# Who makes the low parts of w_out's first three slabs: from VectorE to GpSimd, behind its queries of batches 5 to 7

## The chip, the cores and the metric

One core of a Trainium2 chip runs the whole kernel in one launch. The metric is the device time of that core in microseconds (us), the median of several executions. The engines are TensorE (PE, with its weight loads as PEld), VectorE (DVE), ScalarE (ACT), GpSimd (POOL) and SyncE (SP), which issues the loads from device memory.

## What is computed

A trunk of two layers over 512 prompt tokens and 8 groups of 16 sample tokens (640 rows of 1024). Each layer, cut to what matters here:

```python
h = rms_norm(x, norm_mix); proj = h @ w_in
# o_ret: retention, o_fox: forgetting attention, o_conv: gated short convolution
x = x + concat([o_ret, o_fox, o_conv], -1) @ w_out
x = x + (silu(dwconv3(h2 @ w_gate)) * (h2 @ w_up)) @ w_down      # h2 = rms_norm(x, norm_ffn)

# attention of the sample tokens, for each of 8 batches: 512 cached keys and 16 new ones
sc = einsum('bqhd,bkhd->bhqk', q, k_all) * scale + cq[..., None] - c_t[:, :, None, :]
p = softmax(where(mask, sc, -inf)); o = einsum('bhqk,bkhd->bqhd', p, v_all)
```

## The kernel before, in words

All large products are made of three matmuls (`mm3`): each operand is split into a high part, rounded to fp32r, and a low part, the remainder. Weights arrive in slabs of 128x1024 f32 in three buffers `raw` (slab n in slot n % 3). ACT rounds a slab into `whi` (`split` of ACT, line 1156, semaphore `hi_split`), DVE subtracts that from `raw` into `wlo` (`split` of DVE, line 1538, semaphore `lo_split`), and PE multiplies. Both have `upto(n)`, which makes all slabs up to n that are still missing. SP loads the next slab of a slot when `lo_split` says that the low part of the one before is done. `WO` = 28 is the first of eight slabs of w_out, and `SLOTS` = 3.

The change lies in the sample steps, between the prompt's attention and w_out. For batch n the work goes round the engines:

- POOL, `queries(b, u)`: puts the 16 queries of batch b in block form into `qbd` (two buffers). It waits until the scores of batch b - 2 are complete (`("ss", b - 2)` full).
- PE, `turned(n)`: turns the cached keys of batch n by transposes in four groups of four (`keys_turned`, through three PSUM banks, so the fourth group needs the bank of the first), then the exponentials of batch n - 1 (`ps`), then the remaining part with the output `ob` of batch n - 2. `scores(n)` is the product of `qbd` with the 16 new keys `fkT` and with the 512 turned keys `kT`; `values(n)` is the product of the probabilities of batch n - 1 with the cached values.
- DVE, `step(n)`: two key copies (`key_copy`, L1936) that free PSUM banks; copies out of the bank `po` (L1977, L1981); the masked scores with their running extreme for the old and the new keys (L1997); the smaller of the two extremes (L2001, both operands columns of `small` in SBUF), which releases ACT through `smax`; for the batch before, the sum of the exponentials (L2005), its reciprocal (L2007) and the scaled output `ob` (L2011). In steps 5, 6 and 7 the low part of one slab of w_out follows (lines 2013 to 2015).
- ACT, `step(n)`: two other key copies and the turned probabilities `pTs` (L1252), then the exponentials (L1385). In steps 4, 5 and 6 the high part of one slab of w_out follows.
- SP: cached keys and values of the next batches (1 MB each, lines 757 and 761) as buffers come free, then the slabs of w_out from the fourth on.

`whi` and `wlo` share memory with the cached keys and values of batches 2 and 3 (`kx`, `vx`, `ky`); the wait for `("so", 2)`, the complete output of batch 2, protects that. On PE, `out_slab(0)` follows the steps directly, with the last two `turned` and `values` between the first slabs. The order on each engine is written out by hand and the engines are tied by semaphores. The DVE and ACT lines in question:

```python
if n in (5, 6, 7):                 # DVE, end of step(n)
    B.wait_full(dve, ("so", 2), l)
    upto(WO + n - 5, l)
if n in (4, 5, 6):                 # ACT, end of step(n), behind the exponentials
    B.wait_full(act, ("so", 2), l)
    upto(WO + n - 4, l)
```

Of the kernel before, what the change touches and what calls it, by code (L numbers as in the profile page):

```python
# [30 lines left out]
F32 = mybir.dt.float32  # L31
# [3 lines left out]
ALU = mybir.AluOpType  # L35
# [5 lines left out]
SEQ, NB, NS, PAST = 512, 8, 16, 512  # L41
# [21 lines left out]
SLOTS = 3  # L63


FL, CC, CH, CB, WO, G0 = 4, 22, 24, 26, 28, 36
# [304 lines left out]
def build(nc, a):  # L371
    with ExitStack() as ctx:
        sems = {}

        def sem(name):
            sems[name] = ctx.enter_context(nc.semaphore(name))
            return sems[name]

        bank = [ctx.enter_context(nc.psum_tensor(f"bank{i}", [P, 512], F32)) for i in range(8)]
        B = Banks([sem(f"full{i}") for i in range(8)], [sem(f"free{i}") for i in range(8)])  # L380
# [13 lines left out]
        def own(name, shape, dt=F32):  # L394
            t, top[0] = at(name, shape, dt, top[0])
            return t
# [21 lines left out]
        raw = own("raw", [P, SLOTS, 1024])  # L418
# [70 lines left out]
        def key_home(n, p_):  # L489
            return kT[:, p_, :] if n > 0 else k0[:, p_, :] if p_ < 2 else kT[:, p_ - 2, :]  # L490
# [48 lines left out]
        hi_split = sem("hi_split")  # L539
        lo_split = sem("lo_split")  # L540
# [111 lines left out]
        def slot(n):  # L652
            return n % SLOTS
# [17 lines left out]
        def nth(n, l, more=1):  # L671
            return l * EVENTS + (n if n < DLAST else EV_LAST + n - DLAST) + more
# [26 lines left out]
        def apart(eng):  # L699

            eng.sem_inc(parted, 1)
# [285 lines left out]
        def _(pool):  # L987
# [15 lines left out]
            def norm(which, l):  # L1003
                for t in range(TT):
                    pool.wait_ge(sumsq, l * (2 * TT) + which * TT + t + 1)
                    apart(pool)
                    rsqrt(SS + t, VAR + t, RS + t, 1, 1.0 / D, rstd)

            for l in range(DEPTH):
# [53 lines left out]
                def queries(b, u):  # L1063
                    for par in range(2):
                        dst = qbd[64 * par:64 * par + 64, u, :].rearrange("p (c s) -> p c s", c=4)[:, :, 16 * par:16 * par + 16]
                        src = fqT[64 * par:64 * par + 64, :, SEQ + NS * b:SEQ + NS * b + NS]
                        pool.tensor_copy(dst, src)
                    pool.drain().then_inc(q_ready, 1)
# [12 lines left out]
                for b in range(NB):  # L1081
                    if b >= 2:
                        B.wait_full(pool, ("ss", b - 2), l)
                        apart(pool)
                    queries(b, b % 2)

                norm(1, l)
                pool.wait_ge(cat_lo, l * CATS + CATS)
# [59 lines left out]
        def _(act):  # L1148
            split_to = [0]
# [8 lines left out]
            def upto(n, l):  # L1158

                while split_to[0] <= n:  # L1160
                    if split_to[0] >= SLOTS or l == 0:
                        wait_used(act, split_to[0] - SLOTS, l)
                    elif split_to[0] == 0:
                        B.wait_full(act, ("u", "loop", "a4"), l - 1, PAIRS - 2)
                    else:
                        B.wait_full(act, ("d", "end", split_to[0] - 1, TT - 1), l - 1)
                    split(split_to[0], l)
                    split_to[0] += 1
# [76 lines left out]
            for l in range(DEPTH):  # L1245
                split_to[0] = 0

                def evac(key, out, l, it=None, view=None):

                    B.wait_full(act, key, l, it)  # L1250
                    src = bank[B.bank(key)][:, :] if view is None else view(bank[B.bank(key)])
                    act.activation(out, src, ACT.Copy).then_inc(B.free[B.bank(key)], 1)  # L1252
# [121 lines left out]
                def step(n):  # L1374

                    if n < NB:
                        for p_ in (1, 3) if n > 1 else (2, 3) if n == 1 else ():
                            evac(("kt", n, p_), key_home(n, p_), l)
                    if 1 <= n <= NB:
                        evac(("pt", n - 1), pTs[:, (n - 1) % 2, 0:512], l)  # L1380
                    if n < NB:
                        act.wait_ge(smax, l * NB + n + 1)
                        o = SB + 8 * (n % 2)
                        for c0, n_, acc in ((0, PAST, 3), (PAST + NS * n, NS, 4)):
                            act.activation(ps[:, n % 2, c0:c0 + n_], ps[:, n % 2, c0:c0 + n_], ACT.Exp, scale=-1.0,  # L1385
                                           bias=col(o + 2), accum_out=col(o + acc)).then_inc(sexp, 1)
                    if n in (4, 5, 6):
                        B.wait_full(act, ("so", 2), l)
                        upto(WO + n - 4, l)

                for n in range(STEPS):
                    step(n)
# [135 lines left out]
        def _(dve):  # L1528
            split_to = [0]
# [11 lines left out]
            def upto(n, l):  # L1541
                while split_to[0] <= n:
                    split(split_to[0], l)
                    split_to[0] += 1
# [71 lines left out]
            for l in range(DEPTH):  # L1616
# [348 lines left out]
                def step(n):  # L1965
                    if n < NB:
                        for p_ in (0, 2) if n > 1 else (0, 1) if n == 1 else ():
                            key_copy(n, p_)
                    if n == 1:
                        heads_lo(3)  # L1970
                    if n >= 1:
                        key = ("po", n)
                        bk = bank[B.bank(key)]
                        B.wait_full(dve, key, l)
                        if n <= NB:
                            dve.memset(ps[:, (n - 1) % 2, PAST + NS * (n - 1):PAST + NS * n], 0.0)
                            ins = dve.tensor_copy(pTs[:, (n - 1) % 2, 512:640], bk[:, 0:P])  # L1977
                        if n >= 2:
                            for par in range(2):
                                src = bk[64 * par:64 * par + 64, P:2 * P].rearrange("p (c s) -> p c s", c=4)  # L1980
                                ins = dve.tensor_copy(os_[64 * par:64 * par + 64, :, NS * (n - 2):NS * (n - 1)],  # L1981
                                                      src[:, :, 16 * par:16 * par + 16])
                        ins.then_inc(B.free[B.bank(key)], 1)
                    if n < NB:
                        o = SB + 8 * (n % 2)
                        if n == 0:
                            dve.wait_ge(bnew_ready, l + 1)
                            B.wait_full(dve, ("ss", 0), l)
                            for u in range(2):
                                dve.memset(ps[:, u, PAST:], 0.0)  # L1990
                            dve.drain()
                        for key, c0, n_, c_, bias in ((("ss", n), 0, PAST, 0, pbias[n % 4][:, :]),
                                                      (("sn", n), PAST + NS * n, NS, 1, bnew[:, n, :])):
                            if c_ == 0:
                                dve.wait_ge(pb_in[n % 4], l * 32 + 16 * (n // 4 + 1))
                            B.wait_full(dve, key, l)
                            dve.tensor_tensor_reduce(out=ps[:, n % 2, c0:c0 + n_], in0=bank[B.bank(key)][:, 0:n_], in1=bias,  # L1997
                                                     scale=-1.0, scalar=HUGE, op0=ALU.add, op1=ALU.min,
                                                     accum_out=col(o + c_)).then_inc(B.free[B.bank(key)], 1)
                        dve.drain()  # L2000
                        dve.tensor_tensor(col(o + 2), col(o), col(o + 1), ALU.min).then_inc(smax, 1)  # L2001
                    if 1 <= n <= NB:
                        o = SB + 8 * ((n - 1) % 2)
                        dve.wait_ge(sexp, l * 2 * NB + 2 * n)
                        dve.tensor_tensor(col(o + 5), col(o + 3), col(o + 4), ALU.add)  # L2005
                        dve.drain()
                        dve.reciprocal(col(o + 6), col(o + 5))  # L2007
                        dve.drain()
                        key = ("so", n - 1)
                        B.wait_full(dve, key, l)  # L2010
                        dve.tensor_scalar(ob[:, (n - 1) % 2, :], bank[B.bank(key)][:, 0:P], col(o + 6), None,  # L2011
                                          ALU.mult).then_inc(B.free[B.bank(key)], 1)
                    if n in (5, 6, 7):
                        B.wait_full(dve, ("so", 2), l)
                        upto(WO + n - 5, l)

                for n in range(STEPS):
                    step(n)
# [4 lines left out]
                def add(key, c, t, it=None):  # L2023
# [2 lines left out]
                    dve.tensor_tensor(x[:, t, 512 * c:512 * c + 512], x[:, t, 512 * c:512 * c + 512],  # L2026
                                      bank[B.bank(key)][:, :], ALU.add).then_inc(B.free[B.bank(key)], 1)

                upto(WO + 5, l)
                for t in range(TT):  # L2030
                    add(("wo", 0, t), 0, t)
# [768 lines left out]
```

## Time and profile before

| what | value |
|---|---|
| median of 3 runs | 1594.05 us (1593.94 to 1594.11) |
| profiled execution, its own time | 1593.2 us |
| span of its instructions | 1591.4 us |
| granted TensorE clock | 1.00 |
| PE / PEld busy | 1568.2 us (99%) / 1375.8 us (86%) |
| DVE / ACT / POOL busy | 1073.9 us (67%) / 683.6 us (43%) / 397.8 us (25%) |
| DMA | 168.06 MB, 106 GB/s over the span |

All rows are of one profiled execution; times in them count from the start of its span. The sample steps of layer 1 lie between 266 and 307 us, those of layer 2 between 1054 and 1096 us. Matmuls are pipelined and their ends are modelled, so PE's short waits are read from start times and from the idle time in brackets, not from its busy share. A line number is that of the kernel's code; `split`, `evac` and `mm` are helpers, so their lines serve many places and the names of the tiles tell them apart.

### The profile page before, as it was taken

The numbers are of one execution on the slowest core, as the hardware profiler recorded it, in microseconds if no ns is written. First come the engines' busy times: TensorE is split into PE (matmuls) and PEld (weight loads), VectorE is DVE, ScalarE is ACT, GpSimd is POOL, SyncE is SP. The second block draws the span as 40 slices with busy tenths as digits, with TensorE's granted clock in tenths as the row PEclk, the third lists the DMA queues.
The fourth block names the chain that finished last, engine by engine and source line by source line (L and its number), as shares of the span: only waits on it lengthen the run. The fifth ranks groups of instructions, "written<-read, shape, count | busy, mean of one in ns | idle before, by whom it ended". The sixth has DMA issues, their size and how long they took to land.

```text
span 1591.4 us, 29061 instructions
## 1 busy us (share of the span) xinstructions
PE 1568.2 (99%) x10196; PEld 1375.8 (86%) x10196; DVE 1073.9 (67%) x1847; ACT 683.6 (43%) x1280; POOL 397.8 (25%) x505
## 2 busy tenths in 40 slices
PE   8999999999999999999999999999999999999998
PEld 6878896689999999999888789877899999999997
DVE  4445357539988888888644552674499888878885
ACT  4323337426444444444433233463365444444442
POOL 1113100003433333333112140000043333333330
PEclk9999999999999999999999999999999999999999
DMA  7213455622232222222232225555213222222222
GB/s 233 77 55 84 154 161 193 242 80 67 80 90 82 80 91 88 85 89 67 79 106 67 71 81 183 168 202 198 80 54 118 83 90 80 79 79 79 80 78 72
DMA packets 118872, 168.06 MB, mean 106 GB/s; under 512 B 28261, under 2 KB 80175, under 8 KB 114624
## 3 DMA queue, kind: packets, MB, share of 16 engines
q1 hardware_dynamic: 118648, 166.95, 33.8%
q8 instruction: 49, 0.80, 0.2%
q14 instruction: 29, 0.24, 0.0%
q10 hardware_dynamic: 146, 0.07, 0.0%
HBM read 157.11 MB, written 9.89 MB: 105 GB/s over the span
## 4 chain that ended last, share of the span: by engine, by line
PE 89%; DVE 6%; issue 2%; ACT 1%; DVEq 1%; DMA 0%; POOL 0%; POOLq 0%; SPq 0%; ACTq 0%
PE bank L2239 84%; PE bank L2301 5%; DVE wlo L1552 1%; DVE wlo L1538 1%; DVE x L2026 0%; DVE pf L1898 0%; DVE pf L1911 0%; DVE gact L2056 0%; DVE ps L1997 0%; DVE xn L1590 0%; DVE gulo L1562 0%; DVE xlo L1552 0%; DVE kT L1936 0%; DMA raw<-in_w_up 0%; DMA raw<-in_w_gate 0%
## 5 line engine op out<-in xcount | busy, mean ns | idle before, releaser
L2239 PE MATMUL bank<-whi,hhi 128*128 128x512 f32 x560 | 225.1, 402 | 1.1 <-DVE hlo L1562 0.6
L2239 PE MATMUL bank<-whi,hlo 128*128 128x512 f32 x560 | 219.2, 391 | 0.0
L2239 PE MATMUL bank<-wlo,hhi 128*128 128x512 f32 x560 | 218.7, 390 | 0.0
L2239 PE MATMUL bank<-hhi,whi 128*128 128x320 f32 x640 | 198.7, 310 | 0.8 <-DVE hlo L1562 0.8
L2239 PE MATMUL bank<-hhi,wlo 128*128 128x320 f32 x640 | 197.8, 309 | 0.0
L2239 PE MATMUL bank<-hlo,whi 128*128 128x320 f32 x640 | 197.6, 309 | 0.0
L1538 DVE TENSOR_TENSOR wlo<-raw,whi 128x1024 fp32r<-128x1024 f32 x80 | 100.1, 1251 | 109.6 <-ACT whi L1156 108.2
L2239 PE MATMUL bank<-whi,guhi 128*128 128x512 f32 x440 | 171.7, 390 | 0.4 <-DVE gulo L1562 0.4
L2239 PE MATMUL bank<-wlo,guhi 128*128 128x512 f32 x440 | 171.3, 389 | 0.0
L2239 PE MATMUL bank<-whi,gulo 128*128 128x512 f32 x440 | 171.3, 389 | 0.0
L2026 DVE TENSOR_TENSOR x<-x,bank 128x512 f32<-128x512 f32 x220 | 142.8, 681 | 28.9 <-PE bank L2239 27.0
L2239 PEld LDWEIGHTS bank<-whi,hhi 128*128 128x128 f32 x560 | 105.5, 188 | 25.7 <-issue 3.3
L1156 ACT ACTIVATE whi<-raw 128x1024 fp32r<-128x1024 f32 x80 | 84.4, 1057 | 95.9 <-PE bank L2239 87.3
L2239 PEld LDWEIGHTS bank<-whi,hlo 128*128 128x128 f32 x560 | 105.4, 188 | 22.9
L2239 PEld LDWEIGHTS bank<-wlo,hhi 128*128 128x128 f32 x560 | 105.8, 189 | 20.0
L2239 PEld LDWEIGHTS bank<-hhi,whi 128*128 128x128 f32 x640 | 120.2, 188 | 2.7 <-issue 1.9
L2239 PEld LDWEIGHTS bank<-hlo,whi 128*128 128x128 f32 x640 | 120.2, 188 | 0.8
L2239 PEld LDWEIGHTS bank<-hhi,wlo 128*128 128x128 f32 x640 | 120.1, 188 | 0.0
L1121 POOL TENSOR_TENSOR s<-raw 128x512 f32<-128x512 f32 x60 | 89.8, 1497 | 84.3 <-DMA raw<-in_w_gate 84.3
L1121 POOL TENSOR_TENSOR s<-raw,gains 128x512 f32<-128x512 f32 x20 | 26.9, 1347 | 311.8 <-DMA raw<-in_w_up 301.8
L2239 PEld LDWEIGHTS bank<-whi,gulo 128*128 128x128 f32 x440 | 82.6, 188 | 17.3
L2239 PEld LDWEIGHTS bank<-whi,guhi 128*128 128x128 f32 x440 | 82.6, 188 | 17.3 <-DVE gulo L1562 0.9
(310 smaller groups left out, 3606.4 us busy)
## 6 DMA issues: line engine op xcount, KB each, us to landing
raw<-in_w_in SPq DMA_DIRECT2D x52, 512.0 KB, 3.9
raw<-in_w_gate SPq DMA_DIRECT2D x44, 512.0 KB, 3.8
raw<-in_w_down SPq DMA_DIRECT2D x44, 512.0 KB, 3.5
vb<-in_cache_fox_v SPq DMA_DIRECT2D x14, 1024.0 KB, 6.8
raw<-in_w_up SPq DMA_DIRECT2D x24, 512.0 KB, 3.8
gains<-in_w_up SPq DMA_DIRECT2D x20, 512.0 KB, 3.8
raw<-in_w_out SPq DMA_DIRECT2D x16, 512.0 KB, 4.5
kb<-in_cache_fox_k SPq DMA_DIRECT2D x6, 1024.0 KB, 4.9
```

Of the source, the lines that this page charges most:

```text
L1121: pool.tensor_tensor(by_k(out[:, :]), x_, y_, op).then_inc(s_sum, 1)
L1156: act.activation(whi[:, slot(n), 0:width(n)], raw[:, slot(n), 0:width(n)], ACT.Copy).then_inc(hi_split, 1)
L1538: dve.tensor_tensor(wlo[:, s_, 0:w_], raw[:, s_, 0:w_], whi[:, s_, 0:w_].bitcast(F32), ALU.subtract).then_inc(lo_split, 1)
L1552: dve.tensor_tensor(by_k(part(False, s_)), src, by_k(part(True, s_).bitcast(F32)), ALU.subtract).then_inc(lo_split, 1)
L2026: dve.tensor_tensor(x[:, t, 512 * c:512 * c + 512], x[:, t, 512 * c:512 * c + 512], bank[B.bank(key)][:, :], ALU.add).then_inc(B.free[B.ba ...
L2239: return pe.matmul(out, lhsT=lhsT, rhs=rhs, start=start, stop=stop, skip_group_check=True)
L2301: ins = pe.transpose(dst, src, ident[0:src.shape[0], 0:src.shape[0]])
```

## The change

In the sample steps POOL makes the low parts of slabs 28, 29 and 30, each behind `queries(b)` of b = 5, 6, 7, with a wait for the high part ahead of it. ACT makes each high part ahead of the exponentials of its step. DVE's three low parts in steps 5 to 7 are gone; ahead of its next slabs DVE waits until POOL's three are done.

```diff
@@ gpsimd
                     queries(b, b % 2)
+                    if b >= NB - SLOTS:
+                        n = WO + b - (NB - SLOTS)
+                        pool.wait_ge(hi_split, nth(n, l))
+                        pool.tensor_tensor(wlo[:, slot(n), :], raw[:, slot(n), :], whi[:, slot(n), :].bitcast(F32),
+                                           ALU.subtract)
+                        pool.drain().then_inc(lo_split, 1)
@@ scalar, step(n)
                         evac(("pt", n - 1), pTs[:, (n - 1) % 2, 0:512], l)
+                    if n in (4, 5, 6):
+                        B.wait_full(act, ("so", 2), l)
+                        upto(WO + n - 4, l)
                     if n < NB:
                         act.wait_ge(smax, l * NB + n + 1)
                         o = SB + 8 * (n % 2)
                         for c0, n_, acc in ((0, PAST, 3), (PAST + NS * n, NS, 4)):
                             act.activation(ps[:, n % 2, c0:c0 + n_], ps[:, n % 2, c0:c0 + n_], ACT.Exp, scale=-1.0,
                                            bias=col(o + 2), accum_out=col(o + acc)).then_inc(sexp, 1)
-                    if n in (4, 5, 6):
-                        B.wait_full(act, ("so", 2), l)
-                        upto(WO + n - 4, l)
@@ vector, step(n)
                                           ALU.mult).then_inc(B.free[B.bank(key)], 1)
-                    if n in (5, 6, 7):
-                        B.wait_full(dve, ("so", 2), l)
-                        upto(WO + n - 5, l)
@@ vector, behind the steps
+                dve.wait_ge(lo_split, nth(WO + SLOTS - 1, l, SLOTS + 1))
+                split_to[0] = WO + SLOTS
                 upto(WO + 5, l)
```

## Rows read from the trace of the kernel before

**Rows 1.** The page: the chain that ended last, shares by engine.

```profile
PE 89%; DVE 6%; issue 2%; ACT 1%; DVEq 1%; DMA 0%; POOL 0%; POOLq 0%; SPq 0%; ACTq 0%
```

**Rows 2.** Stretches: length, busy PE, PEld, DVE, ACT, POOL, clock, DMA share, GB/s.

```profile
281.89:287.01 5.12, 4.99 (x79) 3.73 (x78) 3.45 (x14) 2.67 (x9) 0.46 (x2) 1.00 0.71 246
287.01:292.49 5.48, 5.00 (x79) 3.73 (x78) 3.36 (x14) 3.20 (x9) 0.46 (x2) 1.00 0.90 299
292.49:299.05 6.56, 5.09 (x79) 3.90 (x79) 4.49 (x15) 3.92 (x10) 0.47 (x2) 1.00 1.01 350
299.05:305.31 6.26, 5.00 (x80) 3.74 (x79) 4.49 (x15) 3.62 (x10) 0.00 (x0) 1.00 0.68 242
1075.76:1080.88 5.12, 4.99 (x79) 3.73 (x78) 3.45 (x14) 3.19 (x9) 0.47 (x2) 1.00 0.92 294
1080.88:1087.45 6.57, 5.09 (x79) 3.90 (x78) 4.49 (x15) 3.93 (x10) 0.47 (x2) 1.00 1.01 325
1087.45:1093.71 6.26, 5.00 (x80) 3.74 (x79) 4.49 (x15) 3.62 (x10) 0.00 (x0) 1.00 0.82 293
```

**Rows 3.** Timeline, PE, step 5: start, us, what, [idle before it, who ended it].

```profile
297.84 0.63 PE L2301 MATMUL bank<-const,kb 128*128 128x128 f32 x4 [1.27 <-DVE kT L1936]
```

**Rows 4.** Timeline, DVE, steps 3 and 5 of layer 1.

```profile
284.16 0.16 DVE L2001 TENSOR_TENSOR small<-small 128x1 f32<-128x1 f32 x1
...
284.97 1.43 DVE L1936 COPY kT<-bank 128x512 f32<-128x512 f32 x2
...
288.40 0.69 DVE L1997 CUSTOM_DVE_ANT_0 ps<-bank,pb 128x512 f32<-128x512 f32 x1 [0.62 <-PE bank L2239]
...
295.87 1.22 DVE L1538 TENSOR_TENSOR wlo<-raw,whi 128x1024 fp32r<-128x1024 f32 x1
297.01 1.28 DVE L1936 COPY kT<-bank 128x512 f32<-128x512 f32 x2
```

**Rows 5.** Timeline, ACT, step 4 of layer 1.

```profile
286.96 0.59 ACT L1252 ACTIVATE pTs<-bank 128x512 f32<-128x512 f32 x1
...
290.85 1.04 ACT L1156 ACTIVATE whi<-raw 128x1024 fp32r<-128x1024 f32 x1
```

**Rows 6.** Timeline, POOL, step 4 of layer 1.

```profile
288.42 0.51 POOL L1067 COPY qbd<-fqT 64x64 f32<-64x64 f32 x2 [4.62 <-PE bank L2239]
```

**Rows 7.** Timeline, DVE and POOL, in one turn of the loop.

```profile
600.01 1.38 DVE L1552 TENSOR_TENSOR wlo<-s,whi 128x512 fp32r<-128x512 f32 x1
...
610.93 2.47 DVE L2026 TENSOR_TENSOR x<-x,bank 128x512 f32<-128x512 f32 x4
...
630.93 0.69 DVE L1552 TENSOR_TENSOR xlo<-raw,xhi 128x512 fp32r<-128x512 f32 x1
...
599.46 1.38 POOL L1121 TENSOR_TENSOR s<-s,raw 128x512 f32<-128x512 f32 x1 [0.32 <-issue]
...
612.21 1.30 POOL L1121 TENSOR_TENSOR s<-raw 128x512 f32<-128x512 f32 x1 [4.12 <-DMA raw<-in_w_gate]
```

**Rows 8.** Timeline, DVE and POOL, start of layer 2.

```profile
793.72 1.22 DVE L1538 TENSOR_TENSOR wlo<-raw,whi 128x1024 fp32r<-128x1024 f32 x1
793.80 1.19 POOL L999 TENSOR_SCALAR small<-small 128x1 f32<-128x1 f32 x1 [1.83 <-ACT xn L1229]
```

**Rows 9.** POOL's two-operand forms: by group (mean ns), then by line (min/median/max).

```profile
L1025 POOL TENSOR_TENSOR gs<-gs,gng 128x256 f32<-128x256 f32 x5 | 3.5, 735 | 4.8 <-ACT gs L1270 4.8
...
L1121 POOL TENSOR_TENSOR s<-raw x60: 1277/1300/2548, 379.4 to 1541.6; 128x512 f32<-128x512 f32 x60
...
L1039 POOL TENSOR_TENSOR lcdl<-lc,lcd x2: 1533/1534/1534, 142.7 to 931.1; 128x256 fp32r<-128x256 f32 x2
```

**Rows 10.** Batch 7's keys, layer 2: issue, size and time to landing, first use.

```profile
1080.33 0.33 SPq L757 DMA_DIRECT2D kbo<-in_cache_fox_k  x1
...
kbo<-in_cache_fox_k SPq DMA_DIRECT2D x1, 1024.0 KB, 8.4
...
1089.71 1.53 PE L2301 MATMUL bank<-const,kbo 128*128 128x128 f32 x12
```

## The prediction

> **What bounds the kernel now.** The page comes first: TensorE (PE) is busy 99% of the span (the table above), and it makes up 89% of the chain that ended last, so a change to VectorE (DVE), ScalarE (ACT) or GpSimd (POOL) pays only where PE stands and waits for them [rows 1]. The shares hide such places: in the sample steps PE's matmuls are modelled as long ones, and its short idle times vanish in a busy share of 99%. So the second view is the busy time by stretch, with one stretch for each sample step. I call S(n) the moment at which PE begins the scores of batch n (the small product with fkT) and step n the time from S(n) to S(n+1). Undisturbed, a step takes 5.12 us (step 3; the layer-2 step 4 too). Step 4 of layer 1 takes 5.48, step 5 6.56, step 6 6.26; in layer 2 steps 5 and 6 take 6.57 and 6.26 [rows 2]. DVE is busy 4.49 us in the long ones and 3.45 in the short ones, PE 5.0 to 5.1 in both. From S(4) to S(7) it is 18.30 us in layer 1 and 5.12 + 6.57 + 6.26 = 17.95 in layer 2, against 3 x 5.12 = 15.36.
>
> The timeline of PE says what ends the wait in a long step: the last group of four key transposes stands idle for 1.27 us until DVE's key copy [rows 3]. It needs the PSUM bank that this copy frees. The timeline of DVE says why the copy is late: the low part of a w_out slab, 1.22 us, stands directly ahead of it, 295.87 to 297.01 (it sits behind the `ob` scaling at the end of step(n), and the copies open step(n+1)) [rows 4]. In the undisturbed step the copy starts at 284.97, that is S(3) + 3.08, and the minimum of the two column maxima (line 2001, whose operands are both columns of `small` in SBUF) is done at 284.16 + 0.16 = 284.32, S(3) + 2.43 [rows 4]. This order matters: max, minimum, reciprocal, `ob`, key copy stand on DVE one behind the other, and PE has no slack against them, since 1.14 us more ahead of the copy (6.26 - 5.12) came out as a step longer by 1.14. Whatever delays the minimum therefore delays PE by as much.
>
> **The change, part by part.**
> 1. Removed from DVE: three low parts a layer. Those of steps 5 and 6 were on the path; the one of step 7 was not, since PE already multiplies w_out's first slab then. Without them, and with nothing in their place, the four disturbed steps would go back to 5.12. That is worth 18.30 - 15.36 = 2.94 us in layer 1 and 17.95 - 15.36 = 2.59 in layer 2, up to 5.5 us in all.
> 2. Moved on ACT: the high part, 1.04 us, from behind the exponentials to ahead of them, directly behind the evacuation of the turned probabilities (286.96 + 0.59 = 287.55 in step 4) [rows 5]. ACT is idle there until DVE's minimum, so it costs nothing; if that cover were gone it would cost up to 1.04 a step. The slab's data were loaded long before, and its wait (batch 2's output full) is an event of step 3. The high part is then done at 287.55 + 1.04 = 288.59, S(4) + 1.58, instead of 291.89. Its old place pushed a key copy of ACT, by 0.3 us at most, which is within the 2.94.
> 3. Added on POOL: one 128x1024 subtraction behind queries 5, 6 and 7. Behind it on POOL stand queries(6) and queries(7). The wait for the high part of slab 0 holds POOL from 283.8 (its row at 288.42 is queries(6)) to 288.6, and the subtraction then to 291.0, so queries(6) land at about 291.5 instead of 288.9 [rows 6]; PE needs them at S(6), after 299. The same distance holds for queries(7). No cost.
> 4. The price of that subtraction: the trace has no 128x1024 operation on POOL. Plain two-operand rows are 0.735 us at 256 elements and 1.30 at 512 [rows 9], a slope of 0.565 per 256, so 1024 would be 1.30 + 2 x 0.565 = 2.43; I take 2.4. The lower bound is 1.30 itself. The upper bound is the row that writes fp32r, as this one will: 1.53 at 256 elements, four times that is 6.1 us [rows 9]. I stay at 2.4, because that fp32r row ran beside a low part of DVE, the condition of the next point. Each 0.1 us here is 0.6 us in the sum (three steps, two layers).
> 5. What POOL does to DVE meanwhile. In the loop a DVE subtraction with both operands in SBUF takes 0.69 alone and 1.38 when it starts at 600.01 beside a POOL one that runs from 599.46 to 600.84: it ends at 601.39, 0.55 behind POOL's end, so it did nothing until then and only 0.14 of its start lay under the wait [rows 7]. Four adds with one operand in PSUM kept their 0.62 each beside POOL's subtraction at 612.21 [rows 7]. So DVE's max (PSUM and SBUF), the scaling of `ob` and the key copies (PSUM) go on, while operations with two SBUF operands stand until POOL is done. In a step the latter are two only, of one element a partition each: the minimum (L2001) and the sum of the exponentials (L2005). No row shows so small a DVE operation against a long POOL one. The nearest is the other way round: POOL's one-element scaling, begun at 793.80 inside a DVE low part, took 1.19 and ended at 794.99, just behind DVE's 793.72 + 1.22 = 794.94 [rows 8]. One element is no exemption there. The bounds are nothing and the whole rest of POOL's subtraction; I take the second, to which both rows are nearest.
>
> The Trainium skill, "SBUF — State Buffer", section "SBUF: two separate sides", speaks against this change: it calls the port pair of the two engines an exclusive lock, held by whichever starts first for the whole instruction, by a DVE operation if it has two SBUF inputs, and it makes no exception for size. By that rule the sum is the one below; without it, it would be that of the first rival.
>
> Working of one step, step 4 of layer 1: POOL starts at 288.6 and ends at 288.6 + 2.4 = 291.0. DVE's max began at 288.40 and is through at 289.2; the minimum is due at S(4) + 2.27 = 289.28, in the middle of POOL's time [rows 4]. It ends at 291.0 + 0.02 (0.16 less the 0.14 under the wait) = 291.02 instead of 289.44, a delay of 1.58. The exponentials, the sum, reciprocal, `ob` and the key copy follow with their old distances, and PE's last key group waits: 5.12 + 1.58 = 6.70. ACT, PE and POOL keep this phase in the next step, since POOL's start hangs on the high part, which hangs on PE's transposes at S(n). Three steps (4, 5, 6) are hit: 3 x 6.70 = 20.10. Layer 1: 20.10 - 18.30 = +1.80. Layer 2: 20.10 - 17.95 = +2.15. Sum +3.95 us. Note that step 4 had no low part before: DVE loses two delays of 1.14 a layer and gets three of 1.58.
>
> 6. The moved wait and the queues: DVE's new wait for POOL's last subtraction stands behind the last head rows; POOL is done at S(6) + 4.0, before S(7), so it costs nothing. SP moves no transfer ahead or back; its loads of w_out's slabs 3 to 5 wait for the low parts (the third is now done earlier than DVE's old one in step 7) and for the last value load, which is later by about 1.4 us in layer 1, as everything of step 6. They are used only after three slabs of PE work. Nothing.
> 7. Behind S(7) the order is as before, and PE is dense again, so what the steps lose stays lost.
>
> The profiled execution took 1593.2 us with a span of 1591.4; the median of the runs is 1594.05, so 0.85 above it. The sum is a difference and I add it to the median: 1594.05 + 3.95 = 1598.0.
>
> **The rivals.** A change below 0.2% (3.2 us) can't be told from none here.
> - A, faster: the one-element operations of DVE are not held. For it: none was ever seen held, and they read almost nothing. Against it: the two rows of point 5. Then the four long steps go to 5.12. In layer 2 a new bound stands right there: batch 7's keys are issued at 1080.33 and take 8.4 us, to 1088.7, while the transposes that read them, now at 1089.71, would begin at 1080.88 + 5.12 + 2.26 = 1088.26, so 0.45 is lost [rows 10]. 2.94 + 2.14 = 5.1, or 4.7 if the extra 0.36 of step 4 is no effect of ACT: 1589.1. The point from which it decides is the duration of the minimum's row: 0.16 or about 1.7. Chance 0.12.
> - B, slower still: DVE's max is held too, or holds POOL. It runs from 288.40, ahead of POOL, so POOL would start at 289.0 and everything shift by 0.4 more: 6 x 0.4 = 2.4, 1600.4. Against it are the four adds with a PSUM operand [rows 7]. Chance 0.06.
> - C, much slower: the fp32r output makes POOL's subtraction 6.1 us. 3.7 more in each of six steps, 22 us, 1620. Chance 0.02.
> - D, no change to be told: the mechanism of the forecast, but POOL's subtraction 2.2 us or shorter, or part of the delay hidden because PE's wait had some slack. 6 x 0.2 less and below: +0.5 to +3.2, about 1596. Chance 0.13.
> - The forecast as worked out, +3.2 to +5.2: 0.67.
>
> **The numbers.** Slower by over 0.2%: 0.67 + 0.06 + 0.02 = 0.75. Within: 0.13. Faster: 0.12. The range leaves out A, C and the lowest part of D: from 1595.6 (+1.5) to 1600.9 (+6.9, which takes in B and a subtraction of 2.6 us). The price of POOL's subtraction sets its width.
>
> **What would show it.** In the changed profile the POOL rows of the new line should last 2.4 us and start some 1.6 behind S(n); the rows of L2001 in steps 4 to 6 should be 1.7 us long instead of 0.16 and end with POOL's; the waits table should list ACT's exponentials behind `small` L2001 longer by 1.6 in three steps a layer; steps 4 to 6 should be near 6.70, the others 5.12; no DVE low part between S(5) and S(7). A row of 0.16 for L2001 beside a running POOL makes the forecast wrong (A). Steps of 6.70 with a short L2001 would mean another cause.

## The result and the profile after

The changed kernel takes 1597.12 us (median of 20 runs, 1595.14 to 1598.99) against 1593.85 us for the kernel before, run beside it (median of 20, 1592.91 to 1595.06). The ratio is 1.0019, with a 95% interval of 1.0012 to 1.0025: slower, since the interval leaves out 1, by 3.3 us. That is just about the 0.2% that the prediction called the least that can be told. Forecast were 1598.0 us and +3.95, with a range from 1595.6 to 1600.9.

The profiled execution is one of the shorter ones, 1595.64 us with a span of 1593.9. Its page, busy time and chain by engine and by line:

```profile
PE 1567.6 (98%) x10196; PEld 1375.3 (86%) x10196; DVE 1075.1 (67%) x1841; ACT 684.0 (43%) x1280; POOL 414.8 (26%) x511
...
PE 93%; DVE 4%; issue 1%; ACT 1%; DVEq 0%; POOL 0%; POOLq 0%; DMA 0%; SPq 0%; ACTq 0%
PE bank L2244 88%; PE bank L2306 5%; DVE small L2007 1%; DVE pf L1904 0%; DVE pf L1917 0%; DVE xn L1596 0%; DVE ps L2003 0%; DVE kT L1942 0%; DMA raw<-in_w_gate 0%; ACT xn L1235 0%; DVE gulo L1568 0%; DVE ob L2017 0%; POOL small L1001 0%; DVE x L2029 0%; ACT hhi L1213 0%
```

DVE has six instructions fewer and is busy 1.2 us longer. And a line stands in the chain that the chain of the kernel before does not list: `small` L2007, the minimum of two columns of one element (L2001 before). The sample steps by stretch, from S(n) to S(n+1), columns as in [rows 2]:

```profile
281.93:287.05 5.12, 4.99 (x80) 3.73 (x79) 3.44 (x14) 2.67 (x9) 0.46 (x2) 1.00 0.69 244
287.05:293.68 6.63, 4.99 (x80) 3.73 (x79) 4.51 (x14) 3.61 (x10) 2.83 (x3) 1.00 0.93 318
293.68:300.31 6.63, 4.99 (x80) 3.73 (x79) 4.87 (x14) 3.61 (x10) 2.83 (x3) 1.00 0.97 359
300.31:306.94 6.63, 5.00 (x80) 3.73 (x79) 4.86 (x14) 3.62 (x10) 2.36 (x1) 1.00 0.47 163
1076.71:1083.34 6.63, 4.98 (x79) 3.73 (x78) 4.87 (x14) 3.61 (x10) 2.83 (x3) 1.00 0.91 322
```

Steps 4, 5 and 6 take 6.63 us each in both layers, where [rows 2] have 5.48, 6.56, 6.26 and 5.12, 6.57, 6.26. DVE's busy time in such a step is 4.87 with 14 instructions (4.51 in step 4 of layer 1, for a reason given below), more than the 4.49 with 15 that it had when it made the low part itself. The timelines of POOL, ACT, DVE and PE in step 5 (start, us, what, idle before) say why:

```profile
295.24 2.37 POOL L1089 TENSOR_TENSOR wlo<-raw,whi 128x1024 fp32r<-128x1024 f32 x1 [3.50 <-ACT whi L1162]
297.86 0.50 POOL L1067 COPY qbd<-fqT 64x64 f32<-64x64 f32 x2 [0.26 <-issue]
...
294.10 1.06 ACT L1162 ACTIVATE whi<-raw 128x1024 fp32r<-128x1024 f32 x1
297.65 0.72 ACT L1394 ACTIVATE ps<-ps,small 128x512 f32<-128x512 f32 x1 [2.50 <-DVE small L2007]
...
295.06 0.69 DVE L2003 CUSTOM_DVE_ANT_0 ps<-bank,pb 128x512 f32<-128x512 f32 x1 [0.62 <-PE bank L2244]
...
295.67 0.17 DVE L2003 CUSTOM_DVE_ANT_0 ps<-bank,bnew 128x16 f32<-128x16 f32 x1
...
295.94 1.68 DVE L2007 TENSOR_TENSOR small<-small 128x1 f32<-128x1 f32 x1
297.54 0.14 DVE L2011 TENSOR_TENSOR small<-small 128x1 f32<-128x1 f32 x1
...
298.27 1.28 DVE L1942 COPY kT<-bank 128x512 f32<-128x512 f32 x2
...
299.10 0.63 PE L2306 MATMUL bank<-const,kb 128*128 128x128 f32 x4 [1.64 <-DVE kT L1942]
```

POOL's subtraction runs from 295.24 to 297.61. The minimum begins at 295.94 and ends at 297.62, so one element took 1.68 us, and its end is POOL's end; over the six subtractions it ends 0.01 to 0.02 us behind. Everything behind it on DVE follows at the old distances; PE, which stood 1.27 us for the key copy with the low part ahead [rows 3], now stands 1.64. DVE's max has one operand in PSUM. Its large part began 0.18 us ahead of POOL and keeps its 0.69; its small part, for the new keys, begins 0.44 us inside POOL's run, at 295.67, and keeps its 0.17. By line, over all six subtractions and all sixteen minima (ns min/median/max):

```profile
L1089 POOL TENSOR_TENSOR wlo<-raw,whi x6: 2361/2364/2368, 288.6 to 1091.5; 128x1024 fp32r<-128x1024 f32 x6
...
L2007 DVE TENSOR_TENSOR small<-small x16: 158/160/1675, 269.5 to 1098.9; 128x1 f32<-128x1 f32 x16
```

The held instruction shows here as a long busy one, not as idle time. That is why the waits table has no row of DVE waiting for POOL's subtraction (only ACT's wait for `small` is longer), and the duration of the minimum against its own median tells.

Step 4 of layer 1 has one thing more, in the kernel before and in the changed one:

```profile
289.63 0.16 DVE L2001 TENSOR_TENSOR small<-small 128x1 f32<-128x1 f32 x1 [0.44 <-issue]
...
289.67 1.32 DVE L2007 TENSOR_TENSOR small<-small 128x1 f32<-128x1 f32 x1 [0.45 <-issue]
```

DVE stands idle for 0.44 us ahead of the minimum, where the other steps have 0.09, and nothing in the profile ended that wait. So in the kernel before the minimum began at S(4) + 2.62 and not at S(4) + 2.27, and this makes its 5.48 out of 5.12. The same idle time stands ahead of the same minimum, DVE's 339th instruction, in all twelve profiles of the table below. In the changed kernel it passes while POOL's subtraction would hold the minimum anyway: the row is 1.32 instead of 1.68, and the step is 6.63 like the others. What DVE does in it stays open.

The starts of the small `fkT` product give every step of every run. The table has the three steps in question, the time from S(0) to S(7), and what lies between the two layers' steps and behind the last (all us, one profiled execution each):

| kernel | layer 1: steps 4, 5, 6; S(0) to S(7) | between | layer 2: steps 4, 5, 6; S(0) to S(7) | to the end |
|---|---|---|---|---|
| before | 5.48 6.56 6.25; 39.39 | 749.01 | 5.12 6.57 6.26; 39.39 | 497.71 |
| changed | 6.63 6.63 6.63; 40.98 | 748.67 | 6.64 6.63 6.63; 40.99 | 497.27 |
| e1 one source | 5.46 5.10 5.10; 36.73 | 748.77 | 5.10 5.10 5.11; 36.37 | 498.13 |
| e2 high late | 5.48 5.42 5.43; 37.43 | 749.73 | 5.12 5.43 5.43; 37.09 | 497.61 |
| e3 halves | 5.55 5.55 5.55; 37.73 | 749.26 | 5.54 5.55 5.56; 37.76 | 497.97 |
| e4 fill only | 5.47 5.12 5.12; 36.82 | 748.70 | 5.12 5.48 5.04; 36.75 | 497.99 |
| e5 changed again | 6.63 6.63 6.63; 40.99 | 748.42 | 6.64 6.63 6.63; 41.00 | 497.35 |
| e6 high ahead only | 5.71 6.25 6.25; 39.32 | 748.85 | 5.12 6.25 6.25; 39.07 | 497.54 |
| e7 minimum only | 6.57 6.57 6.57; 40.77 | 748.64 | 6.58 6.57 6.57; 40.78 | 497.99 |
| e8 before, one source | 5.46 6.56 6.24; 39.32 | 748.75 | 5.10 6.56 6.24; 39.31 | 497.61 |
| e9 pointer scalar | 5.59 5.22 5.23; 37.52 | 748.65 | 5.23 5.23 5.23; 37.17 | 497.29 |
| e10 one source again | 5.46 5.10 5.11; 36.73 | 748.69 | 5.11 5.11 5.11; 36.38 | 497.61 |

From before to changed the steps add 1.59 + 1.60 = 3.19 us. The long stretches outside them differ between two executions of one kernel too, by up to 0.25 us (changed and e5) and up to 0.52 us (e1 and e10); here they take back 0.34 + 0.44, which, with 0.04 ahead of S(0), makes the span's +2.45. The medians' +3.27 is close to the steps' sum.

### The profile page after: what moved, and what is told of

It is laid out like the page before. It is cut to its first block, busy times and chain, and to the rows that moved or that the text cites. A ratio compares the mean times of both kernels' runs of the same rounds, so it can differ in the third digit from the quotient of the medians.

```text
span 1593.9 us, 29063 instructions
## 1 busy us (share of the span) xinstructions
PE 1567.6 (98%) x10196; PEld 1375.3 (86%) x10196; DVE 1075.1 (67%) x1841; ACT 684.0 (43%) x1280; POOL 414.8 (26%) x511
## 4 chain that ended last, share of the span: by engine, by line
PE 93%; DVE 4%; issue 1%; ACT 1%; DVEq 0%; POOL 0%; POOLq 0%; DMA 0%; SPq 0%; ACTq 0%
PE bank L2244 88%; PE bank L2306 5%; DVE small L2007 1%; DVE pf L1904 0%; DVE pf L1917 0%; DVE xn L1596 0%; DVE ps L2003 0%; DVE kT L1942 0%; DMA raw<-in_w_gate 0%; ACT xn L1235 0%; DVE gulo L1568 0%; DVE ob L2017 0%; POOL small L1001 0%; DVE x L2029 0%; ACT hhi L1213 0%
## 5 line engine op out<-in xcount | busy, mean ns | idle before, releaser
L1544 DVE TENSOR_TENSOR wlo<-raw,whi 128x1024 fp32r<-128x1024 f32 x74 | 92.8, 1254 | 109.7 <-ACT whi L1162 108.5
```

The source lines that it names most:

```text
L1544: dve.tensor_tensor(wlo[:, s_, 0:w_], raw[:, s_, 0:w_], whi[:, s_, 0:w_].bitcast(F32), ALU.subtract).then_inc(lo_split, 1)
```

## The experiments

Theory: while POOL's subtraction runs, DVE operations with two SBUF operands stand still until it ends, whatever their size; the minimum (or the sum behind it) stands ahead of the key copy on DVE, and PE waits for that copy. Rivals: the time goes to POOL's new wait, to the moved high parts on ACT, to slower DVE work in general beside POOL, or to the exponentials that start late.

**e1, one SBUF operand in place of two.** The edit, on the changed kernel:

```diff
-dve.tensor_tensor(col(o + 2), col(o), col(o + 1), ALU.min).then_inc(smax, 1)
+dve.tensor_reduce(col(o + 2), col(o, 2), X, ALU.min).then_inc(smax, 1)
-dve.tensor_tensor(col(o + 5), col(o + 3), col(o + 4), ALU.add)
+dve.tensor_reduce(col(o + 5), col(o + 3, 2), X, ALU.add)
```

> The changed kernel, but in each sample step of VectorE the minimum of the two column maxima and the sum of the two exponential sums are made as reductions over two neighbouring columns, so that they have one SBUF operand instead of two; same values. Theory (GpSimd's subtraction holds only VectorE operations with two SBUF operands): the minimum's row stays near 0.16 us beside the running subtraction, steps 4 to 6 go from 6.63 to 5.12 us, layer 1 from 19.89 to about 15.4 and layer 2 the same or 0.4 more (batch 7's keys land late): about 4.5 a layer less than the changed kernel, 1589 us, ratio to the kernel before 0.9965 to 0.9975. Rival (any VectorE operation that reads SBUF waits, or the step is long for another reason, such as the new wait on GpSimd or the order on ScalarE): steps stay near 6.6, 1597 us.

Measured: 1588.31 us against 1595.16, ratio 0.9958 (0.9944 to 0.9971). POOL and DVE in step 5, and all minima by line:

```profile
296.12 2.37 POOL L1089 TENSOR_TENSOR wlo<-raw,whi 128x1024 fp32r<-128x1024 f32 x1 [2.31 <-ACT whi L1162]
...
296.82 0.15 DVE L2007 TENSOR_REDUCE small<-small 128x1 f32<-128x2 f32 x1
296.90 0.15 DVE L2011 TENSOR_REDUCE small<-small 128x1 f32<-128x2 f32 x1
...
L2007 DVE TENSOR_REDUCE small<-small x16: 154/155/156, 271.6 to 1092.2; 128x1 f32<-128x2 f32 x16
```

Same place, same values, same subtraction of 2.37 us beside it, and no row above 0.156. The steps fall from 6.63 to 5.10; only step 4 of layer 1 keeps 5.46, by the idle time ahead of its minimum:

```profile
291.72 0.15 DVE L2007 TENSOR_REDUCE small<-small 128x1 f32<-128x2 f32 x1 [0.44 <-issue]
```

Nothing else of the change costs anything in the steps, and this version beats both kernels, by a little more than the 0.9965 to 0.9975 expected. The form of the instruction is not what counts: DVE's adds at L2026 are TENSOR_TENSOR as well, with one operand in PSUM, and the 87 of them that began inside one of POOL's operations at L1121 in the kernel before take 0.68 us like the others.

**e2, the same POOL work at another time.** ACT's high parts back behind the exponentials, where the kernel before had them:

```diff
-                    if n in (4, 5, 6):
-                        B.wait_full(act, ("so", 2), l)
-                        upto(WO + n - 4, l)
                     if n < NB:
                         act.wait_ge(smax, l * NB + n + 1)
                         ...
+                    if n in (4, 5, 6):
+                        B.wait_full(act, ("so", 2), l)
+                        upto(WO + n - 4, l)
```

> The changed kernel with ScalarE's high parts put back behind the exponentials; GpSimd still makes the three low parts. Theory: the high part is done 4.9 us behind S(n) instead of 1.6, so GpSimd's 2.36 us end about 2.2 behind S(n+1), just ahead of the minimum (due at 2.27), and hold nothing. Steps 4 to 6: 5.12, 5.4 and 5.4 (0.3 for ScalarE's key copy behind the high part), against 6.63 three times: about 3.9 us a layer less than the changed kernel; 1590 us, ratio to the kernel before 0.997 to 0.9985. Rival (the work costs its time wherever it lies, as GpSimd and VectorE share a path): steps near 6.6 as in the changed kernel, 1597 us.

Measured: 1589.80 us, ratio 0.9971 (0.9959 to 0.9984). POOL, DVE and PE in step 6 (which begins at 299.60):

```profile
299.07 2.37 POOL L1089 TENSOR_TENSOR wlo<-raw,whi 128x1024 fp32r<-128x1024 f32 x1 [2.29 <-ACT whi L1162]
...
302.17 0.16 DVE L2007 TENSOR_TENSOR small<-small 128x1 f32<-128x1 f32 x1
...
300.06 1.07 PE L2244 MATMUL bank<-kT,qbd 128*32 128x512 f32 x8 [0.20 <-issue]
```

POOL ends at 301.44, 0.7 ahead of the two-operand minimum, and nothing is held. The steps are 5.43, and 5.48 or 5.12 for step 4. The 0.3 a step against e1 is ACT's key copy behind the high part, which makes PE's product with `kT` start 0.46 behind S(6) instead of 0.15. So moving the high parts ahead, the half of the change meant to bring POOL's start forward, is what put POOL's work on top of the minimum.

**e3, two halves.**

```diff
-pool.tensor_tensor(wlo[:, slot(n), :], raw[:, slot(n), :], whi[:, slot(n), :].bitcast(F32), ALU.subtract)
+for h in (0, 512):
+    pool.tensor_tensor(wlo[:, slot(n), h:h + 512], raw[:, slot(n), h:h + 512],
+                       whi[:, slot(n), h:h + 512].bitcast(F32), ALU.subtract)
```

> The changed kernel with GpSimd's subtraction of 1024 elements cut into two of 512. Theory (a held operation starts when the running GpSimd instruction ends, not before): the first half runs from 1.56 to 2.85 behind S(n), the minimum ends at about 2.87 and its row lasts 0.6 instead of 1.68. The sum of the exponentials follows 0.08 later; if the second half is ahead of it, it is held to about 4.2 and the key copy with it, so the step is still about 6.6 to 6.8 (1597 to 1598 us); if it slips in ahead, the step is about 5.6 (1591 us). Rival (the delay is no lock, but slower VectorE work in proportion to GpSimd's): the minimum's row stays near 1.7.

Measured: 1590.47 us, ratio 0.9972 (0.9962 to 0.9983). Step 5:

```profile
294.39 2.51 POOL L1090 TENSOR_TENSOR wlo<-raw,whi 128x512 fp32r<-128x512 f32 x2 [2.26 <-ACT whi L1163]
...
295.10 0.59 DVE L2008 TENSOR_TENSOR small<-small 128x1 f32<-128x1 f32 x1
295.61 0.15 DVE L2012 TENSOR_TENSOR small<-small 128x1 f32<-128x1 f32 x1
...
296.34 1.28 DVE L1943 COPY kT<-bank 128x512 f32<-128x512 f32 x2
```

The minimum ends at 295.69, which is 1.30 behind POOL's start and so the end of the first half [rows 9]: it is let go at the end of the first of two POOL instructions. The sum behind it is through as well: its row begins 0.02 ahead of that of the second half and ends 0.13 inside it. So the second half held neither, the better of the two outcomes that were expected. POOL's total grew by 0.14 and the step is 5.55: it lost 0.43 instead of 1.5.

**e4, a fill in its place.** The low parts of w_out's first three slabs are left out (zero), so its time shows the change without its price.

```diff
-pool.tensor_tensor(wlo[:, slot(n), :], raw[:, slot(n), :], whi[:, slot(n), :].bitcast(F32), ALU.subtract)
+pool.memset(wlo[:, slot(n), :].bitcast(F32), 0.0)
```

> The changed kernel with a fill by zero in place of GpSimd's subtraction: the low parts of w_out's first three slabs are left out (zero). It is the bound: the change with nothing of its price. Theory: a GpSimd operation that reads no SBUF, and is over about 2.6 us behind S(n), holds the minimum by 0.15 us at most; steps 4 to 6 are 5.12 to 5.3 in layer 1; in layer 2 one of the later steps is up to 0.4 longer, because batch 7's keys land late. 1589 us, ratio 0.9965 to 0.9975. Rival (the new wait of GpSimd for the high part, or ScalarE's order, lengthens the steps): 6.6 a step as in the changed kernel, 1597 us.

Measured: 1589.06 us, ratio 0.9968 (0.9956 to 0.9980). Step 5 of layer 1:

```profile
295.58 0.95 POOL L1089 MEMSET wlo<- 128x1024 f32 x1 [3.76 <-ACT whi L1161]
...
296.31 0.16 DVE L2006 TENSOR_TENSOR small<-small 128x1 f32<-128x1 f32 x1
```

The fill runs until 296.53; the two-operand minimum begins and ends inside it and is not held (so in five of six; in step 4 of layer 1 it came behind the fill). So not every POOL instruction holds it. The fill writes the same tile as the subtraction but reads none, which points at POOL's reading; no other instruction of POOL was tried. POOL's wait for the high part is free. In layer 2, step 5 is 5.48 and step 6 5.04. Batch 7's keys did not do that: they are turned in step 6. PE stood in step 5 behind the key transposes, among those of the exponentials:

```profile
1084.05 0.60 PE L2305 MATMUL bank<-const,ps 128*128 128x128 f32 x4 [0.20 <-issue]
```

Nothing in the profile ended that wait, and e1 has 5.10 there; its cause stays open.

**e5, the changed kernel once more**, beside e6 to e8.

> The changed kernel once more, on the chip of this group, to stand beside the others: steps 4 to 6 at 6.63 us, +3.5 us in the steps of both layers, 1597 us, ratio 1.001 to 1.003.

Measured: 1597.00 us, ratio 1.0017 (1.0008 to 1.0026), steps 6.63.

**e6, ACT's part alone.** The kernel before with the high parts moved ahead of the exponentials as in the change (the ACT part of the diff), nothing on POOL, low parts on DVE.

> The kernel before with ScalarE's part of the change alone: high parts ahead of the exponentials, low parts on VectorE in steps 5 to 7 as before, GpSimd unchanged. Both theories: ScalarE's own delay of a key copy (0.3 us behind S(5) and S(6)) goes, nothing else. Steps 4, 5 and 6 5.4 (layer 1) or 5.12, 6.26 and 6.26: 0.3 us a layer less than before, 0.6 us in all, ratio 0.999 to 1.000. If the order on ScalarE were part of the loss, it would be slower than before.

Measured: 1593.44 us, ratio 0.9998 (0.9989 to 1.0007), no difference that can be told. In layer 2 the steps gained 0.32, as expected (39.39 to 39.07); in layer 1 only 0.07, since step 4 took 5.71 in this execution: PE's product with `kT` began 0.39 behind S(4) instead of 0.15, and the minimum, with DVE's idle time ahead of it, at S(4) + 2.87. The moved high parts are no part of the loss, and the wait of 1.26 for the low part is still there:

```profile
298.00 0.63 PE L2301 MATMUL bank<-const,kb 128*128 128x128 f32 x4 [1.26 <-DVE kT L1936]
```

**e7, the minimum alone with one operand**, the sum with two (the first half of e1's edit).

> The changed kernel with only the minimum made from one SBUF operand (a reduction over two columns); the sum of the exponentials keeps its two. Theory: the minimum's row is 0.16 and ScalarE's exponentials start on time, but the sum, 0.08 behind, is now the one that is held, to GpSimd's end, and the key copy stands behind it on VectorE: the sum's row lasts about 1.6 and the steps stay at 6.5 to 6.6, so 1597 us, ratio 1.001 to 1.003. If the path went by the exponentials instead, the steps would be near 5.12 and the time near 1588.5.

Measured: 1595.70 us, ratio 1.0011 (1.0002 to 1.0020). Step 5:

```profile
296.81 2.37 POOL L1089 TENSOR_TENSOR wlo<-raw,whi 128x1024 fp32r<-128x1024 f32 x1 [3.44 <-ACT whi L1162]
...
297.51 0.15 DVE L2007 TENSOR_REDUCE small<-small 128x1 f32<-128x2 f32 x1
297.58 1.61 DVE L2011 TENSOR_TENSOR small<-small 128x1 f32<-128x1 f32 x1
...
299.77 1.28 DVE L1942 COPY kT<-bank 128x512 f32<-128x512 f32 x2
```

The sum is now held until 299.19, POOL's end at 299.18, and the steps are 6.57. ACT's exponentials started on time (S(5) + 2.45) and it did not help: the path runs down DVE's own queue to the key copy. Freeing the minimum alone gains 0.06 us a step and freeing both 1.53; the sum alone was not tried.

**e8, control: the two reductions in the kernel before** (e1's edit, POOL as before).

> Control: the kernel before with the two reductions in place of the minimum and the sum; GpSimd as before. Theory: nothing runs beside them, so the steps stay at 5.12, 5.48, 6.56 and 6.26 within 0.02 us each; ratio 0.9995 to 1.0002. If the reductions themselves were what made the earlier run fast, this one would be faster by several us.

Measured: 1593.67 us, ratio 0.9998 (0.9989 to 1.0007), steps 5.46, 6.56, 6.24. Without POOL's subtraction beside them the reductions bring 0.01 us a step, so e1's gain is not theirs.

**e9, a per-partition scalar as the second operand**, also in SBUF:

```diff
-dve.tensor_tensor(col(o + 2), col(o), col(o + 1), ALU.min).then_inc(smax, 1)
+dve.tensor_scalar(col(o + 2), col(o), col(o + 1), None, ALU.min).then_inc(smax, 1)
-dve.tensor_tensor(col(o + 5), col(o + 3), col(o + 4), ALU.add)
+dve.tensor_scalar(col(o + 5), col(o + 3), col(o + 4), None, ALU.add)
```

> The changed kernel with the minimum and the sum made from one SBUF tensor and a per-partition scalar that also lies in SBUF (tensor_scalar). If the scalar is not counted as a second SBUF input, and an operation of one element with one tensor does not take the shared path either, rows stay near 0.16 to 0.3 us, steps 4 to 6 near 5.12, 1588 to 1589 us, ratio 0.995 to 0.997. If what counts is how many addresses in SBUF are read, or the one-tensor form runs in a mode that takes both paths, the minimum's row is 1.7, steps 6.6, 1597 us, ratio above 1.001.

Measured: 1590.83 us, ratio 0.9980 (0.9971 to 0.9989).

```profile
295.22 2.36 POOL L1089 TENSOR_TENSOR wlo<-raw,whi 128x1024 fp32r<-128x1024 f32 x1 [2.46 <-ACT whi L1162]
...
L2007 DVE TENSOR_SCALAR small<-small x16: 212/214/216, 270.1 to 1092.2; 128x1 f32<-128x1 f32 x16
```

None was held, so the scalar does not count as a second operand in this sense. But each row is 0.06 us longer than that of the reduction, beside POOL or not, and two stand on the path in a step: steps of 5.23 instead of 5.10, 0.8 us a layer. That price was not expected (5.12 a step, a ratio of 0.995 to 0.997).

**e10, e1 once more**, beside e9.

> The version with two reductions over neighbouring columns once more, beside the pointer form: steps 4 to 6 at 5.46, 5.10, 5.10, ratio to the kernel before 0.9955 to 0.9975.

Measured: 1587.99 us against 1594.22, ratio 0.9958 (0.9944 to 0.9971): e1's result once more.

## Why the prediction was right, and where it was off

The likeliest case came out: slower, by the mechanism and at the place given. By its points:

- Point 1 (DVE's three low parts gone; the four disturbed steps back at 5.12): right for steps 5 and 6, which are 5.12 in layer 1 of e4 and 5.10 in e1, and wrong for step 4 of layer 1, which had no low part to lose. It stays at 5.47 in e4 and 5.46 in e1, since DVE's idle time ahead of its minimum stays. So steps 4 to 6 gain 2.63 us in layer 1 of e1 and not 2.94; in layer 2 they gain 2.63 (2.59 forecast). This did not touch the sum, because POOL's hold covers that idle time. By medians e1 stands 6.2 to 6.9 us below its runs of the kernel before (e10 and e1), by its profiled steps 2.66 + 3.02 = 5.7; the rest was not placed.
- Point 2 (the moved high part costs nothing): right, e6. In the changed kernel it ended at S(4) + 1.5 (287.47 + 1.06), 0.1 sooner than worked out.
- Point 3 (queries 6 and 7 have time): right, e1. Queries(6) began at 291.23 in the changed kernel, with PE needing them at 300.31.
- Point 4 (2.4 us for the subtraction): 2.36 measured. The fp32r output costs nothing that shows on POOL. Its long row in [rows 9] fits a hold by DVE's low part, which began 0.48 us ahead of it and ended 0.59 us ahead of its end (142.18 to 143.60 against 142.66 to 144.19); no run took that apart. Rival C is out.
- Point 5 (the minimum is held to POOL's end): right to 0.02 us, and the step that carried the forecast. It had been argued from a longer DVE operation and a one-element one of POOL; of the four adds that the prediction sets against them, only the last began inside POOL's run (612.73, and it took 0.68 like the other three). But the changed kernel, e1 and e7 show it for one element of DVE and for either of the two operations, and e4 shows that a fill does not hold. The Trainium skill ("SBUF — State Buffer", section "SBUF: two separate sides") states the two-input condition, that it holds "only against a GpSimd op that reads SBUF", and that the pair is kept for the whole instruction; it names no size. The runs agree with 1.68 against 0.16 us. Rival A is out by the changed kernel's own rows, and rival B by the small max, which begins inside POOL's run and keeps its 0.17 us, and by POOL's start, 0.08 behind the high part as in e2, where no max ran ahead of it.
- The working took step 4 of layer 1 and put its minimum at 289.28; the trace of the kernel before has it at 289.63, so there its end came 1.16 later and not 1.58; against the minimum of an undisturbed step it is 1.51. The forecast of the step's length does not suffer from that, as it hangs on POOL's end.
- The step: 6.70 worked out, 6.63 measured, 0.07 too much. POOL's 0.04 is in it and the rest is its start, at S(n) + 1.56 and not + 1.59. Times six this is 0.42 us of the sum.
- The other 0.35 of the difference between +3.95 and the steps' +3.19 is a term that the sum lacks: step 1 of layer 2 took 5.65 before and 5.31 after. In the kernel before DVE stands idle there for 0.42 us ahead of the scaling of `ob` (1063.21), again with nothing that ended it. The three versions whose DVE keeps its low parts (before, e6, e8) have it there, and the nine others do not, so it goes with the change and is no scatter; its cause stays open.
- The queues (point 6) and what lies behind S(7) (point 7): nothing, as stated. DVE's new wait has no row.
- Rival A's price had one part wrong: batch 7's keys were to cost 0.45 us in layer 2. In e1 they were issued at 1079.14, landed 7.8 us later at 1086.9, and the transposes began at 1087.05; the issue moved ahead with the steps and the load was 0.6 faster than in [rows 10].
- Of what the profile was to show, one thing came out otherwise, beside the 1.32 in step 4 of layer 1: ACT's idle time before the exponentials grew from 1.93 to 2.50 only, since the high part now fills 1.06 of it. A table of waits alone would have made the delay look like little more than a third of what it is.

On the size: +0.25% was forecast and +0.19% (0.12 to 0.25) measured, so whether it is over the bound of 0.2% can't be told. By the medians' +3.27 it is the forecast's own case (+3.2 to +5.2), by the steps' +3.19 the top of rival D (+0.5 to +3.2), and both have the same mechanism.

## What to carry to other kernels

Before work that reads SBUF goes to GpSimd, list what VectorE runs in that stretch with two operands in SBUF, and count a one-element operation as the whole rest of GpSimd's instruction: its length doesn't matter, only whether something waits behind it. Where there are such operations, give them one SBUF operand (two neighbouring columns reduced, e1), place GpSimd's work in the gap between them (e2), or cut it into shorter instructions (e3). A held instruction looked busy in these profiles, so search for rows that are many times their own median, not for idle time.

## What the runs showed of the hardware

- A VectorE operation of one element with two SBUF operands takes 0.16 us alone and ends with the GpSimd subtraction beside it: 1.68 us. With one SBUF tensor of two elements (0.155), or one tensor and a per-partition scalar in SBUF (0.214), it was not held in any of the rows beside the subtraction.
- A GpSimd fill of 128x1024 (0.95 us) did not hold the two-operand minimum that ran inside it (0.16 us, five times).
- Between two GpSimd subtractions, back to back, the waiting VectorE operation was let in, and the next one, which ends 0.07 us behind it, too (e3), six times of six.
- VectorE stood idle for 0.44 to 0.45 us ahead of one fixed instruction of layer 1 (the minimum of step 4) in all twelve profiles, against some 0.09 ahead of the other minima, with nothing recorded that ended it.
- GpSimd's two-operand subtraction of 128x1024 f32 with an fp32r output takes 2.36 to 2.37 us, two of half the size 2.51.
